# First mixer's depthwise conv: GpSimd multiplies its own four chunks' taps, 256 columns at a time

## The reference

```python
ca, cb = jnp.split(zc, 2, axis=-1)
u = ca * jax.nn.sigmoid(cb)
u = causal_depthwise_conv(u, dw_w[i], dw_b[i])
c = jax.nn.silu(layernorm(u, conv_ln_g[i], conv_ln_b[i])) @ conv_proj[i]
ga, gb = jnp.split(zg, 2, axis=-1)
merged = jax.nn.sigmoid(ga) * a + jax.nn.sigmoid(gb) * c
x = x + merged @ w_out[i]
```

## Time and profile before

| what | us |
|---|---|
| median of 3 runs (lowest, highest) | 1468.95 (1463.99, 1469.27) |
| the profiled execution's own time | 1469.18 |
| span of the profile | 1467.3 |
| TensorE matmul busy | 1387.8 |
| VectorE busy | 964.2 |
| ScalarE busy | 769.2 |
| GpSimd busy | 142.1 |
| GpSimd's adds (L468), 60 of them | 87.7 |
| ScalarE's products (L630), 120 of them | 53.4 |

### The profile page before, as it was taken

The page is one execution under the profiler, slowest core; times in us unless marked ns, Lnnn a source line. Parts: engine busy times, 40 slices in busy tenths (PEclk is TensorE's granted clock), DMA queues, the critical chain, the costliest instruction groups (busy, mean ns, idle before and its releaser), DMA issues.

```text
span 1467.3 us, 17287 instructions
## 1 busy us (share of the span) xinstructions
PE 1387.8 (95%) x6616; PEld 1135.1 (77%) x6616; DVE 964.2 (66%) x1357; ACT 769.2 (52%) x1181; POOL 142.1 (10%) x166
## 2 busy tenths in 40 slices
PE   6999999849998999999999999999999999999997
PEld 4788778738876788877778878688887887688886
DVE  4767745797867676674777675648775556655543
ACT  4444436858875444443654434466445663544441
POOL 3000102643420010010001000000000000000000
PEclk9999999969999999999999999999999999999999
DMA  8977764613333588875458876455553344465552
GB/s 249 306 255 273 257 196 139 207 43 101 104 127 115 158 266 270 275 257 196 147 178 265 271 265 186 146 162 167 158 144 112 101 147 158 127 187 184 190 184 76
DMA packets 166402, 269.60 MB, mean 184 GB/s; under 512 B 14064, under 2 KB 114584, under 8 KB 166320
## 3 DMA queue, kind: packets, MB, share of 16 engines
q1 hardware_dynamic: 153952, 226.66, 48.7%
q0 software_dynamic: 12064, 41.49, 8.4%
q10 hardware_dynamic: 304, 0.35, 0.1%
HBM read 267.40 MB, written 1.05 MB: 183 GB/s over the span
## 4 chain that ended last, share of the span: by engine, by line
PE 81%; DVE 9%; ACT 5%; DMA 2%; POOL 2%; issue 1%; SPq 0%; DVEq 0%; ACTq 0%; POOLq 0%
PE ps L1557 26%; PE ps L1534 15%; PE ps L1536 15%; PE ps L1535 15%; DVE w_lo L905 2%; POOL y L468 2%; PE ps L1657 1%; ACT w_hi L487 1%; PE ps L1904 1%; DMA raw<-in_ffn_wgu_dram 1%; DMA raw<-in_ffn_wdown_dram 1%; PE ps L1590 1%; PE ps L1676 1%; PE ps L1693 1%; PE ps L1730 1%
## 5 line engine op out<-in xcount | busy, mean ns | idle before, releaser
L905 DVE TENSOR_TENSOR w_lo<-raw,w_hi 128x1024 fp32r<-128x1024 f32 (+2 forms) x431 | 521.6, 1224 | 324.7 <-ACT w_hi L487 323.6
L487 ACT ACTIVATE w_hi<-raw 128x1024 fp32r<-128x1024 f32 (+2 forms) x431 | 450.2, 1053 | 389.3 <-DMA raw<-in_ffn_wgu_dram 114.4
L1534 PE MATMUL ps<-w_hi,a_hi 128*128 128x512 f32 (+1 forms) x1136 | 457.5, 403 | 8.2 <-DVE a_lo L993 3.5
L1536 PE MATMUL ps<-w_hi,a_lo 128*128 128x512 f32 (+1 forms) x1136 | 444.2, 391 | 0.0
L1535 PE MATMUL ps<-w_lo,a_hi 128*128 128x512 f32 (+1 forms) x1136 | 443.6, 390 | 0.0
L1534 PEld LDWEIGHTS ps<-w_hi,a_hi 128*128 128x128 f32 x1136 | 215.5, 190 | 51.6 <-issue 4.4
L1536 PEld LDWEIGHTS ps<-w_hi,a_lo 128*128 128x128 f32 x1136 | 215.0, 189 | 46.1
L1535 PEld LDWEIGHTS ps<-w_lo,a_hi 128*128 128x128 f32 x1136 | 215.7, 190 | 40.9
L1557 PE MATMUL ps<-w_hi,hid_hi 128*128 128x512 f32 x336 | 104.0, 391 | 0.0
L468 POOL TENSOR_TENSOR y<-y,prod 128x512 f32<-128x512 f32 x60 | 87.7, 1462 | 164.4 <-ACT prod L630 160.0
L1557 PE MATMUL ps<-w_hi,hid_lo 128*128 128x512 f32 x336 | 103.5, 389 | 0.0
(11 more groups left out here) (338 smaller groups left out, 1318.9 us busy)
## 6 DMA issues: line engine op xcount, KB each, us to landing
raw<-in_ffn_wgu_dram SPq DMA_DIRECT2D x176, 256.0 KB, 4.0
raw<-in_w_in_dram SPq DMA_DIRECT2D x88, 512.0 KB, 3.6
raw<-in_w_gu_dram SPq DMA_DIRECT2D x176, 256.0 KB, 3.1
ada<-in_w_ada_dram POOLq DMA_DIRECT2D x72, 512.0 KB, 5.4
raw<-in_ffn_wdown_dram SPq DMA_DIRECT2D x44, 512.0 KB, 4.2
raw<-in_w_dn_dram SPq DMA_DIRECT2D x44, 512.0 KB, 3.6
raw<-in_w_in_dram SPq DMA_DIRECT2D x36, 256.0 KB, 3.1
raw<-in_w_out_dram SPq DMA_DIRECT2D x16, 512.0 KB, 3.6
```

Of the source, the lines that this page charges most:

```text
L487: act.activation(w_hi[:, u % RING, 0:nk * n], raw[:, u % RING, 0:nk * n], ACT.Copy).then_inc(hi_ready, 1)
L905: dve.tensor_tensor(w_lo[:, u % RING, 0:nk * n], raw[:, u % RING, 0:nk * n], w_hi[:, u % RING, 0:nk * n].bitcast(F32), ALU.subtract).then_ ...
L1534: pe.matmul(dst(t)[:, 0:n], a[0], slot(u, w_hi, kk, n), start=kc == 0, stop=False)
L1536: i = pe.matmul(dst(t)[:, 0:n], a[1], slot(u, w_hi, kk, n), start=False, stop=kc == KC - 1)
```

## The change

GpSimd's part of the program makes each tap of each chunk in two operations of 256 columns: a multiplication of `uT` by the tap's weight into `prod` (tap 0 goes into `y` with the bias), and an add to `y`. The add waits for its own multiplication (`pool_product`); a multiplication or a first tap waits for the step two back. `pool_step` now counts one per chunk and tap, and TensorE's two waits go by the new counts (62 and 124). GpSimd waits for `par_ready` and for each group's `uT_ready` itself. ScalarE's `products` and its three calls are gone.

```diff
+            n = m = 0
+            pool.wait_ge(sem("par_ready"), 1)
             for g in range(2):
-                c = POOL_CH[g]
-                for k in range(1, TAPS):
-                    j = (TAPS - 1) * g + k - 1
-                    pool.wait_ge(sem("conv_product"), TAP2 * g + 2 * (k + 1))
-                    if j >= 1:
-                        pool.wait_ge(sem("pool_step"), j)
-                    pool.tensor_tensor(y[:, c:c + 2, :], y[:, c:c + 2, :], prod[:, j % 2, :, :], ALU.add).then_inc(sem("pool_step"), 1)
+                c0 = POOL_CH[g]
+                pool.wait_ge(sem("uT_ready"), 2 + 2 * g)
+                for k in range(TAPS):
+                    for c in (c0, c0 + 1):
+                        n += 1
+                        src = uT[:, c, k:k + S]
+                        if k == 0:
+                            if n > 2:
+                                pool.wait_ge(sem("pool_step"), n - 2)
+                            r = ROW[("dw_b", 0)]
+                            pool.tensor_scalar(y[:, c, :], src, par[:, c, 0:1], par[:, c, r:r + 1], ALU.mult, ALU.add).then_inc(sem("pool_step"), 1)
+                            continue
+                        v = prod[:, 0, c - c0, :]
+                        if n > 2:
+                            pool.wait_ge(sem("pool_step"), n - 2)
+                        pool.tensor_scalar(v, src, par[:, c, k:k + 1], None, ALU.mult).then_inc(sem("pool_product"), 1)
+                        m += 1
+                        pool.wait_ge(sem("pool_product"), m)
+                        pool.tensor_tensor(y[:, c, :], y[:, c, :], v, ALU.add).then_inc(sem("pool_step"), 1)
...
-            made = [0]
-
-            def products(n, limit=2 * TAP2):
...
-                if slot >= 7:
-                    products(3, TAP2 if slot < 27 else 2 * TAP2)
...
-                products(6)
-            products(2 * TAP2)
...
-                    pe.wait_ge(sem("pool_step"), TAPS - 1)
+                    pe.wait_ge(sem("pool_step"), TAP2)
...
-            pe.wait_ge(sem("pool_step"), 2 * (TAPS - 1))
+            pe.wait_ge(sem("pool_step"), 2 * TAP2)
```

## The result

The changed kernel takes 1522.6 us (median of 4 runs, 1521.34 to 1523.02) against 1469.11 for the kernel before: a ratio of 1.0368, 95% interval 1.0341 to 1.0395, so 3.7% or 53.5 us slower. The forecast was 1488, in a range up to 1518.

The account below looks back on a forecast made before the run. TensorE was taken to bound the kernel except at holdups such as the conv. GpSimd's last add at 238.98 + 165 + 43 = 447 gave +17, the clock 2 more: 1469.2 + 19 = 1488 us, range 1469 to 1518.

Parts of the forecast that it names:

- What is added to GpSimd: GpSimd's conv work: a tap of one chunk takes 1.36 us, with a 0.50 us multiplication; 165 us in all.
- Rival 2: GpSimd's conv ends last and far out, at 484: multiplication 0.70 us, collisions 55 us; 1525 us, chance 0.17.
- The narrow add: GpSimd's add of 256 columns in the conv, put at 0.70 us, with 0.63 as the least.
- the end goes by the last add: At TensorE's last conv wait: GpSimd's last add ends at 447, moving the end from 430.06, +17 us.
- the 2 us for the lower clock: Behind TensorE's new pause at the conv sums: some 5 us of matmuls at clock 0.72 take 2 us more.
- The collisions' cost to GpSimd: GpSimd held up by VectorE's splits and other two-operand operations during the conv: 43 us, bounds 25 and 55.
- The cost of a busy GpSimd to the attention slots: VectorE's five operations a slot lose 1.5 us, 0.8 of it covered: +10 us over 12 slots, bounds 0 and 32.
- what is removed: ScalarE's products and waits, read at slots 16 to 25: VectorE's split gains 4 us; the rest to cub stays.
- Rival 4: At cub, ScalarE's relief and shorter GpSimd operations gain 4 and another 4 to 6 us; 1460 us, chance 0.13.
- -4 + 2 + 10 = +8: TensorE's arrival at its last conv wait: relief, VectorE's loss before attention and attention slots move it from 430 to 438.

Follow-up runs that it names:

- e13_two_op_timed: The changed kernel with a second operation adding 0.0 in GpSimd's multiplication, timed in rounds: 1476.47 us, ratio 1.0055 to the kernel before.
- e4_22_taps: The changed kernel with GpSimd making only taps 0 to 21 of 31 of its four chunks: 1460.64 us, ratio 0.9936.
- e3_relief: The changed kernel with GpSimd making only the first tap of its four chunks, the other 30 left out: 1451.17 us, ratio 0.988.
- e5_act_load: The kernel before without GpSimd's 60 adds; ScalarE still makes all 124 products and never waits for GpSimd: 1452.98 us, ratio 0.9907.
- e12_narrow: The kernel before with each product added by itself, 256 columns wide, and ScalarE's buffer freed by halves: 1462.28 us, ratio 0.9948.
- e9_no_wait: The kernel before with GpSimd's adds reading the shifted input instead of the products, so ScalarE need not wait for them: 1462.78 us, ratio 0.995.
- e10_pause: The kernel before with ScalarE's products left out of slots 16 to 24 and made later, four in an attention slot: 1468.3 us, ratio 0.9993.
- e7_group_0: GpSimd alone makes chunks 0 and 1 with two-operation multiplications; ScalarE makes products for 4 and 5 from slot 32: 1467.31 us, ratio 0.9999.

## Why the prediction was wrong

**The step that failed** is in "What is added to GpSimd": "bounds are half the narrow add, 0.32 us, and the narrow add itself, 0.70; I take the middle, 0.50". It measured 0.922. With it a tap is the 1.71 us read above and the step's sum 207 us in place of 165; the whole sum is then 237 + 207 + 37 = 481 in place of 447. The number was sound for a two-operation instruction (0.484) and wrong for the one in the diff. The upper bound had a reason, one operand against two, and no row; no row excluded a multiplication dearer than an add, and the range should have said so. The estimate from the Trainium skill, GPSIMD Engine Reference, section Performance versus the Vector engine, was 0.41 to 0.57 us: the trace agrees for the two-operation form and not for the one-operation form. Rival 2, GpSimd last and far out, is what happened. That its end of 484 (480.8 measured) and its 1525 us (1522.6) came so near is luck: its multiplication of 0.70 was 26 us short over 120 and its collisions of 55 were 18 us too many. The range stopped at 1518, short of that rival's own 1525.

**Right by their own steps.** The narrow add (0.70, measured 0.736 in the median). That the end goes by the last add and shifts TensorE's sums one for one, and the 2 us for the lower clock behind the pause: the eight matmuls of the sums (L1833 and L1836) took 1.9 us longer than before, with a granted clock of 0.53 from 481 to 486 us. The collisions' cost to GpSimd (43, measured some 37, and 44 in e13_two_op_timed).

**Right in direction, too large.** The cost of a busy GpSimd to the attention slots, put at +10 us. Column B of the table has +5.5 in the changed kernel and +7.0 in e4_22_taps against the kernel before. The 9.5 us between e3_relief and e4_22_taps are no measure of it: the profiles have some 3 us of that difference ahead of the attention (A), and the forecast's +10 counted from the kernel before, not from a quiet GpSimd. In the changed kernel VectorE's small operations in those slots show the mechanism (groups from 325 to 400 us, mean ns as the second number after the bar):

```profile
L1141 DVE TENSOR_TENSOR st<-st 128x2 f32<-128x2 f32 (+1 forms) x12 | 7.8, 652 | 0.0
...
L1132 DVE TENSOR_TENSOR st<-st,nsink 128x2 f32<-128x2 f32 (+1 forms) x11 | 4.2, 379 | 0.4
...
L1131 DVE TENSOR_TENSOR st<-st,nqs 128x2 f32<-128x2 f32 (+1 forms) x11 | 3.0, 268 | 0.4
```

L1131 is the 202 ns operation of the earlier trace rows, L1132 and L1141 follow it. Against 0.16 us for an operation that meets nothing they lose 0.1, 0.2 and 0.5 us a slot, and the split (mean 1284) some 0.06; together 0.9 us and not the 1.5 put down. Less of it was covered than the 0.8 I had counted on: VectorE's wait for scores (L1130) fell from 9.8 us to 7.0, 0.2 a slot. Size and cover were both off and in part made up for each other.

**Wrong: what is removed.** "The rest to cub at 305.92 is VectorE's own queue and stays." It did not stay. Head sums, a split and cub in the changed kernel, to be held against 286.18, 290.43 and 305.92 in the earlier trace rows:

```profile
278.97 0.42 DVE L1217 TENSOR_REDUCE rt<-qsq 128x4 f32<-128x256 f32 x1
...
282.25 1.23 DVE L894 TENSOR_TENSOR w_lo<-raw,w_hi 128x1024 fp32r<-128x1024 f32 x1 [1.94 <-ACT w_hi L501]
...
292.84 0.87 DVE L1254 SCALAR_TENSOR_TENSOR cub<-ps,rstd,csg 128x256 f32<-128x256 f32 x2
```

Cub began 13.1 us earlier, 10.9 without the lead of 2.2. Of these, 6.0 were won by the split (the step had 4), and 4.9 between the split and cub, in 10.6 us instead of 15.5: the part that was to stay.

The step saw VectorE busy and took busy time for work. Part of it was waiting behind GpSimd's adds. The operation of 36 columns that took 1.066 us took 0.197 in the changed kernel, and the four rope products 0.628 each instead of 0.979 (groups from 240 to 430 us, first the kernel before, then the changed one; without any adds, in e5_act_load, they took 0.452):

```profile
L1247 DVE TENSOR_TENSOR rope<-qkv,const 128x288 f32<-128x288 f32 x4 | 3.7, 979 | 0.0
...
L1236 DVE TENSOR_TENSOR rope<-qkv,const 128x288 f32<-128x288 f32 x4 | 2.3, 628 | 0.0
...
L932 DVE TENSOR_TENSOR rt<-rs 128x36 f32<-128x36 f32 x1 | 0.2, 197 | 0.0
```

Rival 4 named the place and nearly the size (4 and another 4 to 6 us at cub). Its reason, shorter operations, isn't borne out alone: in e12_narrow, where GpSimd's adds are made shorter and its work is otherwise the same, the way from that split to cub still takes 15.0 us, with the rope products at 0.974; VectorE there meets twice as many adds that each hold it half as long. In the changed kernel an add is under way for only 0.72 of each 1.71 us. And rival 4's other condition, attention slots at TensorE's pace, failed (B). Measured from the transposes of the first conv block, TensorE's arrival is 12.1 us earlier by A and 5.5 later by B, 6.6 earlier in all, where the forecast had -4 + 2 + 10 = +8. e4_22_taps arrives at about the same time (422.7), finds GpSimd done, and takes 1460.6. I had also booked the gain to ScalarE's products. e5_act_load shows that these cost nothing with the adds gone, and e9_no_wait that some 6 us were ScalarE's waits and 10 the adds' presence beside VectorE.

**Open.** Why one operation is slower than two on GpSimd isn't known; only the second operation with its constant was varied. Whether the narrow adds gain by shorter holds or by freeing ScalarE's buffer sooner wasn't parted by a run; the traces lean to the buffer, since ScalarE's waits halved and the way from the split to cub got only 0.5 us shorter (15.0 against 15.5). A pause in GpSimd's work whose products are made up without four a slot in the attention wasn't tried. Medians of 4 to 12 runs don't part versions 2 us from each other.

## What to carry to other kernels

Before an engine is given a new instruction, find a row of exactly its form, operand by operand: a row of the same name and shape was there for neither bound, and a second operation with a constant operand decided 46 us. Where two engines share a resource, a busy engine's time is not all work: compare the same small operation with and without the neighbour at work before calling its queue fixed. When work is moved out of a stage, count what it costs where it lands: e10_pause and e7_group_0 gained 9 to 10 us in the head chain and gave them back behind it. And try the neighbour's operations shorter, and buffers freed sooner, even at a cost to it: 120 adds of 256 columns in place of 60 of 512 made GpSimd 14 us busier and the kernel 0.5% faster.

## What was not expected of the hardware

GpSimd's multiplication by a per-partition scalar, 128x256 in float32, takes 0.922 us with one operation and 0.484 with a second one that adds 0.0. While GpSimd made the slow ones, VectorE was held up less than beside the quick ones: the mean of its full-width splits from 240 to 430 us is 1304 ns in the changed kernel (first fence) and 1481 in e13_two_op_timed (second), 1221 in e3_relief, where GpSimd makes first taps only. One split of the changed kernel began at 340.69, with 0.3 us of the multiplication of 340.09 still to run, and took 1.22 us, as with nothing beside it.

```profile
L894 DVE TENSOR_TENSOR w_lo<-raw,w_hi 128x1024 fp32r<-128x1024 f32 x40 | 51.9, 1304 | 8.1 <-ACT w_hi L501 8.0
```

```profile
L894 DVE TENSOR_TENSOR w_lo<-raw,w_hi 128x1024 fp32r<-128x1024 f32 x40 | 59.0, 1481 | 7.5 <-ACT w_hi L501 7.4
```

And 48 us more or less of ScalarE's busy time in the mixer, in front of its weight splits, made no difference that the runs can tell while GpSimd made no adds (1451.17 us with 719.9 busy in e3_relief, 1452.98 with 768.0 in e5_act_load).
